# One fused two-block network: the first head of each pair has its probabilities turned by VectorE in 32x32 blocks, the second head's stay on TensorE

## The reference

```python
def second_block(x, ...):
    h = rmsnorm(x, g_norm)
    a_u, a_v, a_gate, q, k, v, b_gate, gate_logits = split(h @ w_in)
    y_a = chunked_spatial_gating(gelu(a_u), gelu(a_v), w_s, b_s, g_v) * silu(a_gate)
    y_b = dilated_attention(q, k, v) * silu(b_gate)      # 16 heads of 64
    g_a, g_b = split(sigmoid(gate_logits))
    x = x + (g_a * (y_a @ w_proj_a) + g_b * (y_b @ w_proj_b)) @ w_out
    return rmsnorm(x, g_final)
```

## Time and profile before

| what | value |
|---|---|
| median of 3 runs | 1372.03 us (1371.85 to 1372.12) |
| the profiled execution | 1371.71 us, of which the span of the trace is 1369.9 us |
| TensorE busy (matmuls) | 1354.2 us, 99% |
| VectorE busy | 822.0 us, 60% |
| ScalarE busy | 593.7 us, 43% |
| GpSimd busy | 71.3 us, 5% |
| moved by DMA | 126.99 MB, mean 93 GB/s |

### The profile page before, as it was taken

How to read it: one execution, slowest core, us unless ns; L and a number is a source line. 1 busy time by engine, 2 the same in 40 slices (tenths; PEclk the granted TensorE clock), 3 DMA queues, 4 the chain that set the end, 5 groups by cost and what they waited for, 6 DMA issues and landing times.

```text
span 1369.9 us, 17346 instructions
## 1 busy us (share of the span) xinstructions
PE 1354.2 (99%) x6365; PEld 1100.5 (80%) x6365; DVE 822.0 (60%) x1270; ACT 593.7 (43%) x1003; POOL 71.3 (5%) x60
## 2 busy tenths in 40 slices
PE   7999999999999999999999999999999999999998
PEld 6787777778888888888888888877877787778886
DVE  7768888785676544354445453645654655464685
ACT  7435555554554442124333345734433433343234
POOL 1000000102002000000023300000000000000000
PEclk9999999999999999999999999999999999999999
DMA  5333323143333333333333333323232232223232
GB/s 161 93 92 77 78 72 95 60 127 108 93 93 92 93 105 94 99 86 107 92 106 93 92 92 108 96 72 91 77 89 74 82 92 81 81 78 92 83 118 92
DMA packets 224101, 126.99 MB, mean 93 GB/s; under 512 B 21234, under 2 KB 214851, under 8 KB 224034
## 3 DMA queue, kind: packets, MB, share of 16 engines
q1 hardware_dynamic: 222418, 123.47, 31.4%
q10 hardware_dynamic: 1616, 2.62, 0.6%
HBM read 123.98 MB, written 2.10 MB: 92 GB/s over the span
## 4 chain that ended last, share of the span: by engine, by line
PE 96%; ACT 1%; DVE 1%; issue 1%; DMA 0%; ACTq 0%; DVEq 0%
PE lin L642 26%; PE lin L646 25%; PE lin L645 25%; PE ob L1060 1%; PE sc L749 1%; PE sc L725 1%; PE sc L1016 1%; PE sc L1019 1%; PE tr L738 1%; PE sc L1020 1%; PE ob L762 1%; PE tr L1016 1%; PE lin L1016 1%; PE lin L1019 1%; PE tr L1020 1%; PE tr L1019 1%
## 5 line engine op out<-in xcount | busy, mean ns | idle before, releaser
L1652 DVE TENSOR_TENSOR wl<-raw,wh 128x1024 fp32r<-128x1024 f32 (+2 forms) x235 | 288.1, 1232 | 73.2 <-ACT wh L1170 68.3
L1170 ACT ACTIVATE wh<-raw 128x1024 fp32r<-128x1024 f32 (+2 forms) x235 | 238.5, 1022 | 136.2 <-DMA raw<-in_w_mlp_dram 46.1
L642 PE MATMUL lin<-uh,wh 128*128 128x512 f32 x624 | 250.9, 402 | 1.3 <-DVE ul L1705 1.0
L646 PE MATMUL lin<-uh,wl 128*128 128x512 f32 x624 | 243.3, 390 | 0.0
L645 PE MATMUL lin<-ul,wh 128*128 128x512 f32 x624 | 243.1, 390 | 0.0
L642 PE MATMUL lin<-vh,wh 128*128 128x512 f32 x512 | 205.7, 402 | 0.0
L646 PE MATMUL lin<-vh,wl 128*128 128x512 f32 x512 | 200.0, 391 | 0.0
L645 PE MATMUL lin<-vl,wh 128*128 128x512 f32 x512 | 199.4, 389 | 0.0
L642 PEld LDWEIGHTS lin<-uh,wh 128*128 128x128 f32 x624 | 117.2, 188 | 29.1 <-issue 4.3
L645 PEld LDWEIGHTS lin<-ul,wh 128*128 128x128 f32 x624 | 117.3, 188 | 25.6 <-issue 2.9
L646 PEld LDWEIGHTS lin<-uh,wl 128*128 128x128 f32 x624 | 117.1, 188 | 24.8
(11 more groups left out here) (556 smaller groups left out, 2038.8 us busy)
## 6 DMA issues: line engine op xcount, KB each, us to landing
raw<-in_w_in_dram SPq DMA_DIRECT2D x100, 512.0 KB, 3.8
raw<-in_w_mlp_dram SPq DMA_DIRECT2D x64, 512.0 KB, 4.1
raw<-in_w_out_dram SPq DMA_DIRECT2D x16, 512.0 KB, 3.7
raw<-in_w_xkv_dram SPq DMA_DIRECT2D x8, 512.0 KB, 3.9
raw<-in_w_proj_b_dram SPq DMA_DIRECT2D x8, 512.0 KB, 4.1
raw<-in_w_proj_a_dram SPq DMA_DIRECT2D x8, 512.0 KB, 4.0
xtok<-in_x_dram ACTq DMA_DIRECT2D x4, 512.0 KB, 5.1
raw<-in_w_mla_out_dram SPq DMA_DIRECT2D x4, 512.0 KB, 3.5
```

The costliest lines, as they stand in the source:

```text
L642: ins = pe.matmul(o, wh[:, slot, at], xh_, start=start, stop=False)
L646: return pe.matmul(o, wl[:, slot, at], xh_, start=False, stop=stop)
L1170: act.activation(wh[:, c.slot(4), 0:size], raw[:, c.slot(2), 0:size], ACT.Copy).then_inc(hi_made, 1)
L1652: dve.tensor_tensor(wl[:, c.slot(4), 0:size], raw[:, c.slot(2), 0:size], wh[:, c.slot(4), 0:size].bitcast(F32), ALU.subtract).then_inc(lo_ ...
```

## The change

A new tile `first_turned` (10 tiles of 128x128) lies over SBUF that `vtok`, `td` and part of `rbc` use in other stages. Sixteen VectorE transposes a pair, each of ten 32x32 blocks, turn the first head's probabilities from `logit` straight into it. TensorE's ten transposes of that head and the copies that followed them are gone. The first head is weighed tile by tile, ten matmuls of 128 columns, between the four wider ones of the second head. VectorE's list is put in another order, the second head's transposes and the weighing come later in jobs 5 and 6, and one load semaphore near the start is merged with another.

```diff
+        first_turned = sb("first_turned", [P, 10, P], stack=st)
...
             def weigh_pair(g):
-                pe.wait_ge(turned_act, HEADS + 2 * g + 2)
-                pe.wait_ge(turned_dve, 2 * g + 2)
-                for kb in range(QT):
-                    for p in range(2):
-                        rows, at = slice(64 * p, 64 * p + 64), kb * P + 64 * p
-                        ins = pe.matmul(ob[rows, kb * P:S], gb[:, g, at:at + 64], WEIGHTS[p][kb], start=kb == 0,
-                                        stop=kb == QT - 1)
+                pe.wait_ge(blocks_turned, g + 1)
+                pe.wait_ge(turned_act, HEADS + g + 1)
+                pe.wait_ge(turned_dve, g + 1)
+                for q in range(QT):
+                    for kb in range(q + 1):
+                        ins = pe.matmul(ob[0:64, q * P:(q + 1) * P], gb[:, g, kb * P:kb * P + 64],
+                                        first_turned[:, q * (q + 1) // 2 + kb, :], start=kb == 0, stop=kb == q)
+                        if kb == 0:
+                            pe.matmul(ob[64:P, q * P:S], gb[:, g, q * P + 64:(q + 1) * P], WEIGHTS[q],
+                                      start=q == 0, stop=q == QT - 1)
                 ins.then_inc(ob_ready, 1)
...
                 def turn_mixing():
-                    pe.wait_ge(turned_act, HEADS + 2 * g + 1)
+                    wait(pe, logits_made, n1.times(4, 1))
...
-                job(c + 3, j + 3, DT, vh, vl, between={6: lambda: turn_rows(n0, TURNED[0], (0, 1, 2))})
-                job(c + 4, j + 4, DT, vh, vl, between={0: lambda: turn_rows(n0, TURNED[0], (3,))})
-                job(c + 5, j + 5, DT, vh, vl, between={
-                    0: turn_mixing, 4: lambda: turn_rows(n1, TURNED[1], (0, 1, 2)),
-                    6: lambda: turn_rows(n1, TURNED[1], (3,))})
-                job(c + 6, j + 6, DT, vh, vl, between={0: mix, 3: lambda: weigh_pair(g)})
+                job(c + 3, j + 3, DT, vh, vl)
+                job(c + 4, j + 4, DT, vh, vl)
+                job(c + 5, j + 5, DT, vh, vl, between={0: turn_mixing, 7: lambda: turn_rows(n1, TURNED, (0, 1, 2))})
+                job(c + 6, j + 6, DT, vh, vl, between={0: mix, 1: lambda: turn_rows(n1, TURNED, (3,)),
+                                                       6: lambda: weigh_pair(g)})
...
                 split(c + 6)
-                copy_first_keys(n0, 0)
                 evacuated(act, j + 2)
...
-                copy_first_keys(n1, 1)
                 split(c + 8)
+                copy_first_keys(i)
...
+            def turn_blocks(n, *parts):
+
+                probs = logit[:].rearrange("p (t k x) -> p t k x", t=10, k=4)
+                wait(dve, probs_scaled, n.times(4, 4))
+                for k in parts:
+                    for q in range(4):
+                        ins = dve.transpose(first_turned[32 * k:32 * k + 32, :, 32 * q:32 * q + 32],
+                                            probs[32 * q:32 * q + 32, :, k, :])
+                if 3 in parts:
+                    ins.then_inc(blocks_turned, 1)
+                    dve.wait_ge(blocks_turned, (n.static - HEADS) // 2 + 1)
...
                 maxima(n0, banks=FIRST, scored=g + HEADS)
+                mask(n1, 2 * i + 1)
                 scale_probs(n0)
+                turn_blocks(n0, 0)
+                bend(j + 2, g.times(1, 1))
+                turn_blocks(n0, 1)
                 gelu(j + 2, g.times(1, 1), tb[:])
-                mask(n1, 2 * i + 1)
+                turn_blocks(n0, 2, 3)
+                maxima(n1, second_scores_ready, scored=g)
                 lower(c + 6)
-                copy_other_keys(n0, 0)
-                maxima(n1, second_scores_ready, scored=g)
                 dve.wait_ge(silu_tanh, g.times(2, 1))
```

More of the change, by code:

```diff
@@ L241, in build @@
         kt = sb("kt", [P, S])
+        st = ExitStack()
+        first_turned = sb("first_turned", [P, 10, P], stack=st)
+        st.close()
         vtok = sb("vtok", [P, QT, P])
-        ta, tb, tc, td, te = (sb(n, [P, S]) for n in ("ta", "tb", "tc", "td", "te"))
+        td, rbc, ta, tb, tc, te = (sb(n, [P, S]) for n in ("td", "rbc", "ta", "tb", "tc", "te"))
         bias = sb("bias", [P, S])
@@ L281, in build @@
         pts = sb("pts", [P, 640])
-        rbc = sb("rbc", [P, S])
         nlog = sb("nlog", [P, S])
@@ L303, in build @@
         AV_WORK = ((ta, tb), (te, bias))
-        mem_landed, vecs_landed, taps_landed, consts_landed, pos_landed = (
-            sem(n + "_landed") for n in ("mem", "vecs", "taps", "consts", "pos"))
+        mem_landed, vecs_landed, taps_landed, consts_landed = (
+            sem(n + "_landed") for n in ("mem", "vecs", "taps", "consts"))
         x_landed = [sem(f"x{q}_landed") for q in range(QT)]
@@ L332, in build @@
         turned_act, turned_dve = sem("turned_copied_scalar"), sem("turned_copied_vector")
+        blocks_turned = sem("blocks_turned")
         scores_ready, logits_made, probs_made = sem("scores_ready"), sem("logits_made"), sem("probs_made")
@@ L430, in build @@
         H_COPIED = {f: k + 1 for k, f in enumerate(H_ORDER)}
-        TURNED = ([(tr[0], 0), (tr[1], 0), (ob, 0), (tr[1], 384)], [(sc[0], 0), (sc[1], 0), (sc[2], 0), (sc[2], 256)])
-        WEIGHTS = ([qt[:, 0:512], kt[:, 0:384], pts[:, 0:256], kt[:, 384:512]],
-                   [pt[:, 0:512], pt[:, 512:896], pts[:, 256:512], pts[:, 512:640]])
+        TURNED = [(sc[0], 0), (sc[1], 0), (sc[2], 0), (sc[2], 256)]
+        WEIGHTS = [pt[:, 0:512], pt[:, 512:896], pts[:, 256:512], pts[:, 512:640]]
         FIRST_WEIGHTS = ([pa[:, 0:512], pa[:, 512:896], pa[:, 896:1152], pa[:, 1152:1280]],
@@ L488, in _ @@
                     sp.dma_start(qt[64:128, :].bitcast(I32), a["positions"][0].partition_broadcast(64))\
-                        .then_inc(pos_landed, 16)
+                        .then_inc(consts_landed, 16)
                 load(c + m, w_in, 2 * CONV + P * m, DT, P)
@@ L863, in turns @@
             def turns(n, *rows):
-                turn_rows(Idx(n), TURNED[1], rows)
+                turn_rows(Idx(n), TURNED, rows)
             for u in range(HEADS // 2):
@@ L1079, in mix @@
                     pe.wait_ge(atok_placed, g + 1)
-                    pe.wait_ge(turned_dve, 2 * g + 1)
                     pe.wait_ge(wst_placed, g + 1)
@@ L1223, in o_split, with copy_first_keys @@
                 act.activation(oh[:, at, :], ob[:], ACT.Copy).then_inc(o_high, 1)
-            def copy_first_keys(n, p):
-                wait(act, turned_ready, n.times(1, 1))
-                act.activation(WEIGHTS[p][0], TURNED[p][0][0][:], ACT.Copy).then_inc(turned_act, 1)
+            def copy_first_keys(g):
+                act.wait_ge(turned_ready, HEADS + g + 1)
+                act.activation(WEIGHTS[0], TURNED[0][0][:], ACT.Copy).then_inc(turned_act, 1)
             act.wait_ge(start_made, 2)
@@ L1762, in rope_arguments @@
                 r = slice(64, 128)
-                dve.wait_ge(consts_landed, 16)
-                dve.wait_ge(pos_landed, 16)
+                dve.wait_ge(consts_landed, 32)
                 ang, tmp = kt[r, :], logit[r, 0:S]
@@ L2125, in _, with bend, gelu @@
             dve.wait_ge(rbc_made, 1)
-            def gelu(j, k, dst):
+            def bend(j, k):
                 dve.wait_ge(g_square, k)
                 dve.scalar_tensor_tensor(tb[:], ta[:], 1.0 / GELU_A, read(j)[:], ALU.add, ALU.mult).then_inc(g_poly, 1)
+            def gelu(j, k, dst):
                 dve.wait_ge(g_tanh, k)
@@ L2219, in scale_probs, with copy_other_keys @@
                     dve.tensor_scalar(p, p, rden[:, q:q + 1], None, ALU.mult).then_inc(probs_scaled, 1)
[L2221 to L2229, removed]
+            def copy_other_keys(g):
+                dve.wait_ge(turned_ready, HEADS + g + 1)
+                dve.tensor_copy(pt[:, 512:896], sc[1][:, 0:384])
+                dve.tensor_copy(pts[:, 256:640], sc[2][:, 0:384]).then_inc(turned_dve, 1)
+            def turn_blocks(n, *parts):
[8 more added lines that the diff above has]
+                    dve.wait_ge(blocks_turned, (n.static - HEADS) // 2 + 1)
             for i in range(PAIRS):
@@ L2261, in _ @@
                 freed(dve.scalar_tensor_tensor(te[:], ta[:], 1.0, read(j + 4)[:], ALU.add, ALU.mult), j + 4)
-                copy_other_keys(n1, 1)
                 lower(c + 8)
+                copy_other_keys(i)
                 dve.wait_ge(ob_ready, g.times(1, HEADS // 2 + 1))
```

## The result

The changed kernel takes 1402.4 us (median of 4 runs, 1401.96 to 1403.78) against 1371.94 before in the same runs: a ratio of 1.0224, 95% interval 1.0211 to 1.0237. It is 30.5 us slower.

A forecast was written before the change was run, and what follows sets the result against it. TensorE was taken to bound the kernel; per pair - 1.10 (transposes removed) + 0.68 (weighing) + 3.58 (stalls) + 0.1 (pair's end) = + 3.26 us, eight times + 26.1, giving 1398 us, 1.9% slower; range 1381 to 1409.

The forecast's parts named there:

- What bounds, and the two slacks: TensorE bounds; VectorE frees `lin` banks 2.93 us before TensorE opens job 4 and 2.03 us before job 5.
- The price of a transpose: One VectorE transpose of 32 partitions by 320 elements: 0.53 us, bounds 0.40 to 0.55; sixteen a pair, 8.5 us.
- VectorE's timeline: VectorE's new order over one pair: operation to `te` frees job 3's bank at 1080.89, 4.44 us later; mask costs nothing.
- The waits: TensorE stalls for late banks, 1.4 us at job 4's opening and 2.2 at job 5's, together 3.58 a pair.
- The weighing: Ten narrow matmuls between four wide ones, started in list order: 0.68 us more a pair, bounds 0 and 2.2.
- The clock: TensorE's granted clock: forecast is wrong if the waits make it fall; no size given.
- Behind it nothing more is late: After job 5's opening, the second head's probabilities, copies and loads still arrive in time, so no further stall there.
- The rival of a gain below a price of 0.31: Transposes fit VectorE's idle time, job 5's stall vanishes below 0.31 us each: - 0.32 us a pair, 1369; chance 0.07.
- A2 and A3: Narrow first-head matmuls in the weighing, behind B1 in the list; A2 was to start no sooner than B1.
- B1: Wide second-head matmul of 384 columns in the weighing; said to start only when the first wide one ends, at 0.91.

The follow-up runs named there:

- one_transpose: Changed kernel, but from the second pair on only one of the sixteen VectorE transposes is issued: 1369.45 us, ratio 0.998 to the kernel before.
- wide_transposes: Changed kernel with eight transposes of 640 elements instead of sixteen of 320, half the blocks in wrong rows: 1382.43 us, ratio 1.0077 to the kernel before.
- narrow_weigh_only: Kernel before, with only the first head weighed by ten matmuls of 128 columns, from tiles TensorE turned: 1372.42 us, ratio 1.0004.
- te_early: Changed kernel with only VectorE's operation freeing job 3's bank moved ahead of the last eight transposes, maxima and `lower`: 1384.91 us, ratio 1.0095 to the kernel before.
- both_early: te_early, plus `bend` ahead of the first four transposes and gelu's second operation right behind those: 1378.25 us, ratio 1.0046 to the kernel before.
- half_the_transposes: Changed kernel, but from the second pair on only eight of the sixteen transposes are issued: 1369.39 us, ratio 0.9978 to the kernel before.
- all_early: both_early with weighing one step earlier, second head's scaling sooner, mixing input's copy and first head's mask at pair start: 1363.62 us, ratio 0.9942 to the kernel before.
- twice_the_transposes: Changed kernel with each transpose of 320 elements cut into two of 160: 1409.81 us, ratio 1.0277 to the kernel before.

## Why the prediction was right, point by point

- *What bounds, and the two slacks*: right. Both waits are there eight times, at the places named, and one_transpose removes them.
- *The price of a transpose*: 0.53 predicted, 0.52 measured. Rows on 1024 elements and the slope of other operations were enough; wide_transposes confirms the split into 0.19 fixed and 1.03 ns an element. Only below 320 elements it misleads.
- *VectorE's timeline*: from the scaling to the start of `te` 13.8 us predicted (1066.37 to 1080.21), 13.82 measured. The mask cost nothing, as said: it ran while VectorE waited for ScalarE, of which wait 0.22 us is left.
- *The waits*: 1.4 and 2.2 predicted, 1.46 and 2.06 measured; with the 0.11 lost after a wait, and 0.13 at the pair's end (matmuls at 1111.05, 1111.30 and 1111.64, where 0.23 apart is usual), 3.76 against 3.68. The sum of a pair by what was measured is - 1.10 + 0.08 + 3.76 = + 2.74, and the pair grew by 2.78.
- *The weighing*, the term of the sum that was mis-sized: "each starts in the order of the list, as soon as its half is free" gave 0.68, and it is 0.08 (2.38 against 2.30) in the changed kernel and 0.07 alone (narrow_weigh_only). A narrow matmul did not wait for the wide one ahead of it in the list; the lower bound, free halves, was the right end. That made the sum 4.8 us too high.
- *The clock*, named only as what could make it wrong and priced nowhere, so that the sum put it at nothing: it fell in five pairs, 8.1 us. The two misses have opposite signs and partly cancel: 26.1 - 4.8 + 8.1 = 29.4 of 30.5 us. The median is 4 us above the forecast and inside the range, but the sum is nearer than its parts, and that is luck.
- *"Behind it nothing more is late"*: true for the changed kernel, but only because TensorE was itself held up. te_early and both_early show the next wait, 1.0 and 1.7 us a pair by the weight loads, and my own expectation for te_early missed it by 8 us.
- *The rival of a gain below a price of 0.31*: borne out by half_the_transposes, whose eight at 0.52 are as long as sixteen at 0.26, and which is 2.6 us faster than the kernel before. What the rival left out is that a gain is there at the full price too, by another order (all_early).

## What to carry to other kernels

Work that moves from the bounding engine to an idle one is paid for by the chain on that engine, not by its busy share: here, with VectorE busy for 63% of the span, it cost 22 us in the pairs and 8 more by the clock, and with the same work in another order it saved 8. Before moving it, list for each result that the bounding engine needs how long before its use it is ready, put ahead what frees buffers and what is needed soonest, and push into gaps what only has to be there at the end. When one wait is taken away, look for the next in the same list before counting the gain.

## What the runs showed of the hardware

- In these traces matmuls on the two halves of TensorE's array (64 columns of weights each) don't keep the order of the list between halves: A2 and A3 started before B1, which stands ahead of them, and ten narrow matmuls beside four wide ones took 2.38 us where four beside four took 2.30. The rule of the Trainium skill that tiles work independently (TensorEngine Tiling (Array Packing), Key Properties) is the one that the trace bears out; the Trainium skill's rule of strict program order (TensorE: Matmul & The Clock Gate, Part 3) it does not, between halves.
- The granted clock fell to 1.2 GHz in five of eight pairs with TensorE's two waits at 1.5 and 2.1 us, in seven with the longer ones of twice_the_transposes (1.8 and up to 2.4 by the view), and in none of wide_transposes, te_early, both_early and all_early, whose waits are shorter or fewer. A fall behind job 5's opening cost 1.6 us; the three of twice_the_transposes behind job 4's opening cost nothing, because the wait at job 5 took them up. That the waits bring the falls is inferred from these kernels and no run tried it apart. Why three pairs of the changed kernel escaped is open; one_transpose and half_the_transposes, with one such pair each, had the fall in some executions and not in others.
- A VectorE transpose of 32x160 elements takes 0.29 us from start to start, 32x320 0.52, 32x640 0.85 and 32x1024 1.27: close to a straight line, but only from 320 up. The cause of the short ones' lower price wasn't tried apart.
